# A decoder layer in float32: the FFN up-projection as seven block products in place of eight

## The reference, cut to what matters

```python
def conv_glu_ffn(h, w_up, conv_w, conv_b, w_down):
    gate, val = jnp.split(h @ w_up, 2, axis=-1)
    gate = causal_depthwise_conv(gate, conv_w, conv_b)     # width 3 over tokens
    return (jax.nn.silu(gate) * val) @ w_down
...
x = x + conv_glu_ffn(rms_norm(x, ln_ffn[l]), ffn_w_up[l], ...)   # w_up 1024 x 5632, w_down 2816 x 1024
```

## Time and profile before

| | |
|---|---|
| median of 3 runs | 1664.67 us (1662.75 to 1667.59) |
| profiled execution: span from first to last instruction | 1665.5 us |
| matmuls and transposes on TensorE | 8070 |
| busy: TensorE, VectorE, ScalarE, GpSimd | 1629.9, 814.5, 660.4, 75.8 us |
| HBM read, written | 115.77 MB, 4.19 MB |

### The profile page before, as it was taken

One profiled execution on the slowest core, in us unless ns is written; L12 is line 12 of the kernel. 1 busy time (PEld: TensorE's weight loads), 2 busy tenths in 40 slices (PEclk: granted clock), 3 DMA queues, 4 the chain that ended last, 5 costly groups with the idle time before them and its releaser, 6 DMA issues.

```text
span 1665.5 us, 20724 instructions
## 1 busy us (share of the span) xinstructions
PE 1629.9 (98%) x8070; PEld 1314.4 (79%) x8070; DVE 814.5 (49%) x1347; ACT 660.4 (40%) x1192; POOL 75.8 (5%) x148
## 2 busy tenths in 40 slices
PE   6999999999999999999999999999999999999999
PEld 5887777667776678888888888888888888888887
DVE  5315637547786564423443255555434455555332
ACT  5214218566444562533432144434324344433221
POOL 3000221210002100000000000000000000000000
PEclk9999999999999999999999999999999999999999
DMA  5131000001103171000111233332222433332223
GB/s 155 51 52 39 26 14 26 26 14 62 41 26 114 64 252 52 26 1 1 52 45 38 64 101 90 101 100 78 83 95 89 126 102 118 97 102 95 89 100 109
DMA packets 166920, 121.30 MB, mean 73 GB/s; under 512 B 23448, under 2 KB 140456, under 8 KB 166824
## 3 DMA queue, kind: packets, MB, share of 16 engines
q1 hardware_dynamic: 165496, 115.53, 22.7%
q10 hardware_dynamic: 1328, 4.46, 0.7%
HBM read 115.77 MB, written 4.19 MB: 72 GB/s over the span
## 4 chain that ended last, share of the span: by engine, by line
PE 64%; DVE 1%; ACT 0%; issue 0%; DVEq 0%; ACTq 0%
PE tail_b L100 20%; PE tail_b L101 20%; PE tail_b L102 20%; PE tail_b L2456 2%; PE tail_b L2431 1%; PE tail_b L2420 0%; PE tail_b L2443 0%; PE tail_b L2367 0%; DVE tail_wl L2126 0%; PE tail_b L2575 0%; PE tail_b L2491 0%; PE tail_b L2504 0%; DVE tail_xs L2161 0%; DVE tail_pt L2195 0%; ACT tail_xs L1956 0%
## 5 line engine op out<-in xcount | busy, mean ns | idle before, releaser
L2284 DVE TENSOR_TENSOR ff_wl<-ff_wr,ff_wh 128x512 fp32r<-128x512 f32 (+1 forms) x176 | 168.4, 958 | 330.0 <-ACT ff_wh L2066 330.0
L2066 ACT ACTIVATE ff_wh<-ff_wr 128x512 fp32r<-128x512 f32 (+1 forms) x176 | 148.7, 846 | 377.9 <-PE tail_b L102 377.9
L102 PE MATMUL tail_b<-HH,ff_wl 128*128 128x512 f32 x704 | 273.9, 389 | 0.0
L100 PE MATMUL tail_b<-HH,ff_wh 128*128 128x512 f32 x704 | 273.9, 389 | 0.0
L101 PE MATMUL tail_b<-HL,ff_wh 128*128 128x512 f32 x704 | 273.9, 389 | 0.0
L100 PE MATMUL mix_gb<-HH,mix_wh 128*128 128x512 f32 x432 | 179.3, 415 | 0.8 <-ACT XR L549 0.7
L102 PE MATMUL mix_gb<-HH,mix_wl 128*128 128x512 f32 x432 | 170.2, 394 | 0.0
L101 PE MATMUL mix_gb<-HL,mix_wh 128*128 128x512 f32 x432 | 170.2, 394 | 0.0
L100 PE MATMUL tail_b<-tail_wh,HH 128*128 128x512 f32 x384 | 153.9, 401 | 3.2 <-DVEq L2124 1.9
L100 PEld LDWEIGHTS tail_b<-HH,ff_wh 128*128 128x128 f32 x704 | 132.2, 188 | 27.6
L102 PEld LDWEIGHTS tail_b<-HH,ff_wl 128*128 128x128 f32 x704 | 132.2, 188 | 27.5
(11 more groups left out here) (367 smaller groups left out, 2454.5 us busy)
## 6 DMA issues: line engine op xcount, KB each, us to landing
ff_wr<-in_ffn_w_up SPq DMA_DIRECT2D x88, 512.0 KB, 3.6
ff_wr<-in_ffn_w_down SPq DMA_DIRECT2D x88, 256.0 KB, 2.7
mix_wr<-in_w_in SPq DMA_DIRECT2D x26, 512.0 KB, 3.5
mix_wr<-in_xa_wkv SPq DMA_DIRECT2D x16, 512.0 KB, 3.5
XR<-in_x SPq DMA_DIRECT2D x8, 512.0 KB, 6.3
XR<-in_x ACTq DMA_DIRECT2D x1, 4096.0 KB, 19.6
tail_wr<-in_xa_wq SPq DMA_DIRECT2D x16, 256.0 KB, 4.6
tail_wr<-in_xa_wo SPq DMA_DIRECT2D x16, 256.0 KB, 3.4
```

The costliest lines, as they stand in the source:

```text
L100: pe.matmul(out, hi_w, hi_x, start=first, stop=False)
L102: return pe.matmul(out, lo_w, hi_x, start=False, stop=last)
L2066: act.activation(part(FWH[m % FPART], m), part(FWR[m % FRAW], m), ACT.Copy).then_inc(w_hi, 1)
L2284: dve.tensor_tensor(part(FWL[m % FPART], m), part(FWR[m % FRAW], m), part(FWH[m % FPART], m), ALU.subtract)\
```

## The change

The up-projection is seen as a product of 2x2 blocks: tokens in two halves (FRONT, BACK), the inner dimension in two (k blocks 0 to 3 and 4 to 7), and for each `g` two columns of blocks, gate and value. The eight block products of 12 matmuls are replaced by seven of sums of blocks. For each `g`, once for all 1024 tokens:

| product | weights | activations | PSUM bank |
|---|---|---|---|
| 1 | gate, first half (in `WA`) | FRONT, blocks 0 to 3 | A |
| 2 | gate, second half (in `WA`) | FRONT, blocks 4 to 7 | C |
| 3 | sum, first half of `WB` | `T2` | A, added on |
| 4 | sum, second half of `WB` | `T3` | B |
| 5 | `WC`, first half (a sum) | BACK, place of blocks 0 to 3 (a difference BACK - FRONT) | A, added on |
| 6 | `WC`, second half (value, second half) | `T4` | B, added on |
| 7 | `WD` (a sum of all four) | BACK, blocks 4 to 7 | A, added on |

The sums `T2`, `T3`, `T4` of activation blocks are made once, on VectorE (`x_sums`), split by ScalarE, VectorE and GpSimd. All eight row tiles are normalised ahead of the FFN, in the order 0, 4, 1, 5, 2, 6, 3, 7 (`PAIRED`), seven between the units and the eighth after product 1 of `g` = 0. Sums of weight blocks are made for each `g` by four VectorE instructions on 128x512 (`weight_sums`); four split pairs follow (`a_high`/`a_low` to `d_high`/`d_low`). Between products ScalarE reads the A and B banks (`bank_read`: copies to `G[0]`, `V[0]`, `V[1]`, `G[1]`), and VectorE adds banks to those copies (`bank_added`). There is one raw buffer for gate weights (`RG`), one for value weights (`RV`), and one buffer each for `WA` to `WD`.

The hidden value of each `g` and token half is stored to DRAM (`keep`, 256 KB) and read again for the down-projection (`act_load`), together with the down weights (`down_load`, six buffers). The down-projection has the matmuls of before, in four rounds `r`, each of 22 items `s` of 12. Semaphores of `mixers_block` that are cleared early are more than before; 23 semaphores in place of 8 are left to be cleared at the very end.

```diff
+        S23 = place("ff_s23", [P, KT, P], F32, offset=HIGH + 20 * kilo)
+        S4 = place("ff_s4", [P, KH, P], F32, offset=HIGH + 24 * kilo)
+        G = [place(f"ff_g{h}", [P, HT + 2], F32, offset=HIGH + 26 * kilo + 2080 * h) for h in range(2)]
+        RG = place("ff_rg", [P, KT, P], F32, offset=at + 20 * kilo)
+        RV = place("ff_rv", [P, KT, P], F32, offset=at + 24 * kilo)
+        Y = [place(f"ff_y{h}", [P, HT], F32, offset=at + 2 * kilo * h) for h in range(2)]
+        V = [place(f"ff_v{h}", [P, HT], F32, offset=at + 4 * kilo + 2 * kilo * h) for h in range(2)]
+        TH = place("ff_th", [P, HT], F32, offset=at + 8 * kilo)
...
-        X_UNITS = [(0, 0), (1, 0), (2, 0), (0, 1), (1, 1), (2, 1)] + [(t, c) for t in range(3, NT) for c in range(2)]
+        PAIRED = [t + NTH * e for t in range(NTH) for e in range(2)]
+        X_UNITS = [(t, 0) for t in range(NT)] + [(t, 1) for t in PAIRED]
         x_at = {u: m for m, u in enumerate(X_UNITS)}
...
+        x_tr_bank = lambda j, g: bank3[4 + 2 * (j % 2) + g]
+
+        A_BANK = lambda g: bank[g % 2]
+        B_BANK, C_BANK = bank[2], bank[3]
+        down_bank = lambda r, t: bank[4 * (1 - r % 2) + t]
...
         @block.sync
...
+            def gate_weights(g):
+                if g >= NF:
...
+                    sp.wait_ge(o_done, 2 * NT)
+                    sp.wait_ge(w_lo, WF)
+                else:
+                    sp.wait_ge(u_lo, 4 * (g - 1) + 1)
+                    sp.wait_ge(s_made, 4 * g)
+                sp.dma_start(RG[:], a["ffn_w_up"][0][:, g * P:(g + 1) * P].rearrange("(k p) c -> p k c", p=P))\
+                  .then_inc(gate_loaded, 16)
...
+            def value_weights(g):
...
+                else:
+                    sp.wait_ge(u_lo, 4 * (g - 1) + 3)
+                col = D_FF + g * P
+                sp.dma_start(RV[:], a["ffn_w_up"][0][:, col:col + P].rearrange("(k p) c -> p k c", p=P))\
+                  .then_inc(val_loaded, 16)
+
+            def keep(g, h):
+                sp.wait_ge(act_f, 2 * g + h + 1)
+                sp.dma_start(hidden[h, g], Y[h][:]).then_inc(kept[h], 16)
...
+            def act_load(j):
...
+                if j < A_SLOTS:
+                    sp.wait_ge(prod_done, LAST + j // KH + 1)
...
+                if j >= A_SEMS:
+                    sp.wait_ge(act_hi, j - A_SEMS + 1)
+                sp.wait_ge(kept[u], 16 * (k + 1))
+                sp.dma_start(a_slot(j, 2), hidden[u, k]).then_inc(act_loaded[j % A_SEMS], 16)
...
+            def down_load(w):
...
+                if w < W_SLOTS:
+                    sp.wait_ge(prod_done, LAST + 2 * (w // 2) + 2)
+                else:
+                    sp.wait_ge(item_done, w - W_SLOTS + 1)
+                r, k = divmod(w, NF)
+                c = r % 2
+                sp.dma_start(w_slot(w, 2), a["ffn_w_down"][0][k * P:(k + 1) * P, c * NW:(c + 1) * NW])\
+                  .then_inc(down_loaded[w % W_SLOTS], 16)
...
+            gate_weights(0)
+            value_weights(0)
+            gate_weights(1)
+            value_weights(1)
+            for g in range(NF - 1):
+                if g >= 1:
+                    keep(g - 1, 1)
+                gate_weights(g + 2)
+                keep(g, 0)
+                value_weights(g + 2)
+            keep(NF - 2, 1)
+            for j in range(KH):
+                act_load(j)
+            for w in range(2):
+                down_load(w)
+            for w in range(2, 4):
+                down_load(w)
...
+            keep(NF - 1, 0)
...
+            for s in range(ROUNDS * NF - W_FIRST):
+                down_load(s + W_FIRST)
+                if a_at_step(s) is not None:
+                    act_load(a_at_step(s))
+                if s == 2:
+                    keep(NF - 1, 1)
...
+            def x_plain(j):
+                act.wait_ge(transposed, 2 * (NT + j) + 1)
+                act.activation(T3F[:, :, tok(j // 2)], x_tr_bank(j, 0), ACT.Copy).then_inc(b_plain, 1)
+                act.wait_ge(transposed, 2 * (NT + j) + 2)
+                act.activation(HH[quad(1, PAIRED[j])], x_tr_bank(j, 1), ACT.Copy).then_inc(b_hi, 1)
...
+            for i in range(NT + 1):
+                if i >= 1 and i % 2 == 0:
+                    x_plain(i - 1)
+                if i < NT:
+                    x_stats(i)
+                if i >= 1:
+                    x_high(i - 1)
+                if i == 3:
+                    a_high(0)
+            act.preload_act_table_set(EXP_TANH)
+            b_high(0)
+            c_high(0)
+            for g in range(NF + 1):
+                if g >= 1:
+                    f = g - 1
+                    act.wait_ge(prod_done, PRODUCTS * f + 7)
                     if f >= 1:
...
+                    act.activation(G[1][:, 2:HT + 2], A_BANK(f)[:], ACT.Copy).then_inc(bank_read, 1)
+                    taps(f, 1, A_BANK(f)[:])
+                if g < NF:
+                    d_high(g)
+                if g >= 1:
+                    half_tanh(g - 1, 1)
...
+                act.wait_ge(prod_done, PRODUCTS * g + 1)
...
+                act.activation(G[0][:, 2:HT + 2], A_BANK(g)[:], ACT.Copy).then_inc(bank_read, 1)
+                if g < NF - 1:
+                    a_high(g + 1)
+                else:
+                    for j in range(KH):
+                        act_high(j)
+                    for w in range(2):
+                        down_high(w)
+                act.wait_ge(bank_added, 3 * g + 1)
+                taps(g, 0, G[0][:, 2:HT + 2])
+                act.wait_ge(prod_done, PRODUCTS * g + 3)
...
+                act.activation(V[0][:], A_BANK(g)[:], ACT.Copy).then_inc(bank_read, 1)
+                half_tanh(g, 0)
+                act.wait_ge(prod_done, PRODUCTS * g + 4)
...
+                act.activation(V[1][:], B_BANK[:], ACT.Copy).then_inc(bank_read, 1)
+                if g < NF - 1:
+                    b_high(g + 1)
+                    c_high(g + 1)
...
+            def x_low(j, g):
...
+            def x_sums(j):
+                p, cols, here = j // 2, tok(j // 2), quad(0, PAIRED[j])
+                dve.wait_ge(b_plain, p + 1)
+                dve.tensor_tensor(HLF[here], T3F[:, :, cols], x_tr_bank(j - 1, 0), ALU.subtract).then_inc(sum_made, 1)
+                dve.wait_ge(sum_made, 4 * p + 1)
+                dve.wait_ge(b_hi, 3 * p + 3)
+                dve.tensor_tensor(T2F[:, :, cols], x_tr_bank(j, 1), HLF[here], ALU.subtract).then_inc(sum_made, 1)
+                dve.tensor_tensor(T3F[:, :, cols], x_tr_bank(j, 1), T3F[:, :, cols], ALU.subtract).then_inc(sum_made, 1)
+                dve.wait_ge(sum_made, 4 * p + 2)
+                dve.tensor_tensor(T4F[:, :, cols], x_tr_bank(j - 1, 1), T2F[:, :, cols], ALU.subtract).then_inc(sum_made, 1)
+
+            def x_sums_low(j):
+                p, cols = j // 2, tok(j // 2)
+                dve.wait_ge(sum_hi, 4 * p + 1)
+                dve.tensor_tensor(T2L[:, :, cols], T2F[:, :, cols], T2H[:, :, cols], ALU.subtract).then_inc(sum_lo, 1)
+                dve.wait_ge(sum_hi, 4 * p + 4)
+                dve.tensor_tensor(T4L[:, :, cols], T4F[:, :, cols], T4H[:, :, cols], ALU.subtract).then_inc(sum_lo, 1)
...
+            for i in range(NT + 1):
+                if i < NT:
+                    x_add(NT + i)
+                if i >= 1 and i % 2 == 0:
+                    x_sums(i - 1)
+                if i < NT:
+                    x_scale(i)
+                if i % 2 == 1:
+                    x_low(i - 1, 0)
+                    x_low(i - 1, 1)
+                elif i >= 1:
+                    x_low(i - 1, 1)
+                    x_sums_low(i - 1)
+                if i == 3:
+                    a_low(0)
+
+            def weight_sums(g):
...
+                dve.tensor_tensor(S23[:, SECOND, :], RG[:, FIRST, :], RV[:, FIRST, :], ALU.subtract).then_inc(s_made, 1)
+                dve.wait_ge(s_made, 4 * g + 1)
+                dve.tensor_tensor(RV[:, FIRST, :], RV[:, FIRST, :], RV[:, SECOND, :], ALU.add).then_inc(s_made, 1)
+                dve.wait_ge(s_made, 4 * g + 2)
+                dve.tensor_tensor(S23[:, FIRST, :], RV[:, FIRST, :], RG[:, FIRST, :], ALU.subtract).then_inc(s_made, 1)
+                dve.wait_ge(s_made, 4 * g + 3)
+                if g >= 1:
+                    dve.wait_ge(u_lo, 4 * (g - 1) + 4)
+                dve.tensor_tensor(S4[:], RG[:, SECOND, :], S23[:, FIRST, :], ALU.subtract).then_inc(s_made, 1)
...
+            weight_sums(0)
+            b_low(0)
+            c_low(0)
+            for g in range(NF + 1):
+                if g >= 1:
+                    dve.wait_ge(bank_read, 4 * g)
+                    dve.wait_ge(halo_set, g)
+                    half_conv(g - 1, 1)
+                if g < NF:
+                    d_low(g)
+                    weight_sums(g + 1)
+                if g >= 1:
+                    half_gate(g - 1, 1)
+                    dve.wait_ge(bank_added, 3 * g)
+                    half_product(g - 1, 1)
...
```

(123 more changed lines are left out.)

529 lines of the change are left out of this document (261 added, 268 removed).

## The result

The changed kernel takes **1648.42 us** (median of 4 runs, 1646.75 to 1649.90), the kernel before beside it 1663.8 (median of 4): a ratio of 0.9901, 95% interval 0.9886 to 0.9916. It is faster by 15.4 us where the prediction's sum had 36.8. The time lies inside the range of 1611 to 1650, at its slow end; that it does is luck, as neither a rival nor a bound of the range was about what made the difference. The profiled execution spans 1645.2 us, that of before 1665.5. Times are medians of the fast executions: one of the four of e9_hh_next_256, the profiled one, took 1771.32 us at a mean granted clock of 0.85 and is left out, so e9 has a time and no trace to compare.

What follows compares the result with a forecast made beforehand. TensorE was taken as the bound, through its matmul count and new waits; -59.85 (products), -0.4 (transposes), +15.0 (entry), +3.3 (exit), +4.8 (clock) and +0.4 (end) sum to -36.8 us: 1628 us, range 1611 to 1650.

Steps and rivals of the forecast that it cites:

- The removed products: Up-projection: 1848 matmuls in place of 2112, so 264 fewer at 0.2267 us from start to start: -59.85 us.
- Transposes: Four tiles' transposes leave the first down stage (3.95 us) for a new place, where they cost 3.6: net -0.4 us.
- The steady loop: Up-projection, each g: VectorE and ScalarE keep up with TensorE's 19.04 us, with 0.9 to 1.2 us to spare: 0.
- Rival 2: Loop not bound by TensorE: late value loads or longer handoffs cost 0.5 to 1.5 us per g, 1639 to 1660; chance 0.18.
- rival 4: Slower than before: the value load lands late behind the hidden store in SP's queue; 7 us gives 1681; chance 0.06.
- A: FFN entry, first g: product 1 waits for tile 3's low part, starting at 4.9 us where 0.9 was possible: 4.0 us.
- B: FFN entry, first g: product 3 waits for b_low behind tile 7's work and the weight sums: 6.8 us.
- C: FFN entry, first g: product 5 waits for the V[0] copy, queued behind the next g's weight sums: 4.2 us.
- Exit: Last g: product 5 waits while ScalarE splits activations and down weights first: 3.3 us, bounds 1.5 and 6.
- Clock: After the waits at entry and last g, TensorE runs 3.4 us at 1.2 GHz: +4.8 us, bounds 0 and 6.4.
- Rival 1: At the FFN entry, GpSimd's last two low parts hold up VectorE by two times 1.04 us: 1630; chance 0.10.
- Rival 3: Entry and exit cost little: half the forecast waits and no lower clock gives 1614, none at all 1605; chance 0.13.

Runs made afterwards that it cites:

- e9_hh_next_256: The changed kernel with a pad of 448 bytes, putting HH on the next multiple of 256 (50688, not the old 50432): 1633.79 us, ratio 0.9819.
- e1: The changed kernel with a 192-byte pad where HALO was, so XR, HH and HL stand at their addresses of before: 1632.91 us, ratio 0.9809.
- e2: The kernel before with a 64-byte pad ahead of XR, so HH starts 64 past a multiple of 256: 1684.02 us, ratio 1.0122.
- e11: The changed kernel with e1, e6, e8, first weight sums and tile 3 moved ahead, tanh table load and first G[0] copy earlier: 1614.7 us, ratio 0.9703.
- e6: The changed kernel with the last g's activation and down-weight splits put behind the value copies: 1643.34 us, ratio 0.9874.
- e8: The changed kernel with GpSimd's low parts for each pair of row tiles made by VectorE instead: 1645.47 us, ratio 0.9896.

## Why the prediction was right in sign and wrong in size

**The removed products, right in number and wrong in price.** 264 matmuls fewer is what happened. The step that failed is "one product takes 2.72 us, one g 19.04", and with it "the down-projection keeps its 1056": it took the matmul's 0.2267 us of the earlier trace rows over into a kernel in which `HH` and `HL` no longer start at a multiple of 256. I priced the removal of `HALO` at nothing; it isn't named in the prediction at all. With the addresses restored one g is 19.04 (e1), without them 19.28, and the 1152 matmuls of the tail units, which the change does not touch, are slowed with the rest. The missing term is **+15.5 us** (e1 against the changed kernel), three quarters of the 21 us by which I was off. In the kernel before it would be 20 us (e2).

**Transposes: the -0.4 holds to within 0.5 us**, once placement is set right. Down-projection of e1: from 1383.37 to its last matmul's start at 1622.51 and one matmul more, 239.4 us, 3.9 less than before; in the changed kernel placement takes these 3.9 back. The two more bursts among the tail units were to cost 1.8 and cost some 1.4: e1's tail units take 350.01 us for 350.23 before, without the 1.6 us of lower clock that the execution of before has.

**The steady loop costs 0: right.** No wait of TensorE recurs, and e1's g is the 19.04 us of 84 matmuls. Rival 2 falls; the landings of 2.0 and 3.7 us leave nothing for rival 4.

**Entry: 15.0 forecast, 16.1 measured, but shared out otherwise.** A took 5.7 for 4.0, B 9.0 for 6.8, C 1.5 for 4.2. A is longer because VectorE's low parts of T2 and T4 take 2.9 us together beside GpSimd and unit 15's sum waits behind them, to 945.57 us. In B I had product 3 released by `b_low`. ScalarE's rows show another:

```profile
960.70 1.28 ACT L2228 ACT_TABLE_LOAD   x1
965.36 1.06 ACT L2183 ACTIVATE ff_wbh<-ff_s 128x1024 fp32r<-128x1024 f32 x1 [3.38 <-DVE ff_s L2536]
966.32 1.04 ACT L2191 ACTIVATE ff_wch<-ff_rv 128x1024 fp32r<-128x1024 f32 x1
967.27 0.61 ACT L2197 ACTIVATE ff_wdh<-ff_s 128x512 fp32r<-128x512 f32 x1
967.79 0.58 ACT L2249 ACTIVATE ff_g<-tail_b 128x512 f32<-128x512 f32 x1
```

The copy of bank A into `G[0]` (L2249), which product 3 waits for, stands in ScalarE's list behind the two high parts and `d_high`; these wait for the first weight sums. It comes at 967.79. (The first row is the load of ScalarE's tanh table, which e11 moves ahead.) So B holds part of what I had put in C, and C is small. I had checked the order of the VectorE list and not that of ScalarE's at this place.

**Exit: 3.3 forecast, 3.7 measured**, for the reason given: e6 moves the splits and the wait goes.

**Clock: 4.8 forecast, about 6.3 measured.** The stretch view of the changed kernel behind A, behind B and at the last g (granted clock third from last):

```profile
946.00:956.00 10.00, 5.92 (x16) 4.68 (x17) 2.73 (x4) 2.62 (x6) 0.00 (x0) 0.66 0.00 0
957.00:974.50 17.50, 8.54 (x28) 6.60 (x27) 13.39 (x17) 8.04 (x11) 2.93 (x2) 0.71 0.20 60
1386.60:1390.80 4.20, 4.17 (x12) 3.42 (x13) 1.63 (x3) 3.19 (x7) 0.00 (x0) 0.65 0.61 226
```

In these three windows the level of 1.2 GHz was granted for 6.8, 10.2 and 2.9 us (the window's length times what its granted clock lacks to 1.00, times two, as this level is half the clock). Product 1 takes 5.26 us, product 3 takes 5.0 and the last g's product 5 takes 4.21, each for 2.72: 2.5 + 2.3 + 1.5. "Behind B it is hidden by C" was wrong, as C had shrunk. With 1.5 for the waits and 1.5 for the clock, e1's up-projection is 2.8 us over what I had forecast, 446.5 for 443.7.

**End: +0.4 forecast, +1.4 measured**, 5.5 us for 4.1; no run takes it apart.

**Sum of the corrections:** placement 15.5, waits 1.5, clock 1.5, end 1.0 give 19.5 of 21.4; the 1.9 left is no more than the executions of one kernel differ by.

**Rival 1 had a true mechanism and a small price.** I gave it 2 us; e8 finds 0 to 3 by the times and 1.7 by the length of the up-projection. The Trainium skill, SBUF — State Buffer, section SBUF: two separate sides, says that the two engines exclude each other on such operands. The rows above and e8 agree: VectorE's two are lengthened by 0.5 and 1.1 us while GpSimd works beside them.

**Rival 3** (entry and exit cost little) fails for the kernel as written and becomes nearly true by reordering: e11 has 5.6 us of waits for the changed kernel's 19.9.

**What stays open** is how the address acts. The groups of one window of the loop, 1005 to 1380 us of the changed kernel (count; busy us, mean ns of one; idle us):

```profile
L100 PE MATMUL tail_b<-HH,ff_wah 128*128 128x512 f32 x160 | 63.0, 394 | 0.0
...
L100 PE MATMUL tail_b<-ff_t2h,ff_wbh 128*128 128x512 f32 x80 | 31.7, 396 | 0.0
...
L100 PE MATMUL tail_b<-HH,ff_wdh 128*128 128x512 f32 x77 | 30.4, 395 | 0.0
...
L100 PE MATMUL tail_b<-ff_t4h,ff_wch 128*128 128x512 f32 x76 | 30.1, 396 | 0.0
...
L100 PE MATMUL tail_b<-ff_t3h,ff_wbh 128*128 128x512 f32 x76 | 29.6, 389 | 0.0
```

The same of e1:

```profile
L100 PE MATMUL tail_b<-HH,ff_wah 128*128 128x512 f32 x160 | 62.2, 389 | 0.0
...
L100 PE MATMUL tail_b<-ff_t2h,ff_wbh 128*128 128x512 f32 x80 | 31.1, 389 | 0.0
```

Products on `HH` are slow, as expected, but so are those on T2 and T4, whose addresses are the same in both kernels and multiples of 256; those on T3 are not. T2's product follows one on `HH`, and T4's too, T3's follows T2's. From start to start, over ten g, the means are 229.6 ns on `HH` and `HL`, 230.8 on T2 and T4, 226.7 on T3, and 226.7 for all of them in e1. So a product is slowed by the address of a buffer that it does not read; the runs show that and not why. In the down-projection matmuls whose activations lie in `HH` and `HL` start 233 ns apart, those in T2's buffer 227. Nor do the runs tell whether the address itself counts or where `HH` and `HL` lie against the other operands: in every run the FFN's other operands start at multiples of 256 bytes and only `XR`, `HH` and `HL` leave them. Whether `HH` or `HL` matters more, or whether both do, is open too.

## What to carry to other kernels

A buffer removed or added ahead of TensorE's operands is a change of its own: read off at which address they then start, and if a multiple of 256 bytes is lost, expect what was seen here, some 1 to 3% on the matmuls that read them, in stages that the change does not touch too. Where a stage without waits runs at another pace than before, compare start-to-start times of one kind of matmul ahead of looking for a stall. Where a loop is entered, go through each engine's list for the one instruction that TensorE needs first, and see what has been put before it.
